# One-hot columns of the expert gates shared among three engines, with eight up tiles in three split passes beside them

## The reference

```
top_s, top_i = lax.top_k(s, PEER_TOPK)
...
idx = jnp.take_along_axis(cand_i, best_j, axis=-1)
gates = jax.nn.softmax(best_s, axis=-1)
...
uc = u_tab[ic]
vc = v_tab[ic]
hdn = jax.nn.gelu(jnp.einsum('cd,chkd->chk', xc, uc), approximate=False) * gc
return jnp.einsum('chk,chkd->cd', hdn, vc)
```

## Time and profile before

| | us |
|---|---|
| median of 3 runs | 1634.44 (1633.93 to 1637.54) |
| the profiled execution, its own time | 1635.94 |
| span of the profile | 1634.1 |
| PE busy | 1593.3 (98%) |
| DVE busy | 1261.5 (77%) |
| ACT busy | 869.6 (53%) |
| POOL busy | 194.7 (12%) |

### The profile page before, as it was taken

One profiled execution on the slowest core, in us unless ns is written; L12 is line 12 of the kernel. 1 busy time (PEld: TensorE's weight loads), 2 busy tenths in 40 slices (PEclk: granted clock), 3 DMA queues, 4 the chain that ended last, 5 costly groups with the idle time before them and its releaser, 6 DMA issues.

```text
span 1634.1 us, 32308 instructions
## 1 busy us (share of the span) xinstructions
PE 1593.3 (98%) x11274; PEld 1413.1 (86%) x11274; DVE 1261.5 (77%) x2678; ACT 869.6 (53%) x1599; POOL 194.7 (12%) x153
## 2 busy tenths in 40 slices
PE   6999999999999999999999999999999999999998
PEld 4887988899988877888888888888899877999998
DVE  6885647859989888788888888888778465688887
ACT  3444230464569854555555555555654246576665
POOL 0020211026600000000000000000048004300000
PEclk9999999999999999999999999999999999999999
DMA  9842137856641388777777777777545661255554
GB/s 359 291 139 88 41 133 259 308 165 199 205 146 63 102 257 255 233 243 236 232 238 237 237 241 236 239 237 242 186 157 170 206 207 40 79 174 185 181 180 128
DMA packets 102623, 316.85 MB, mean 194 GB/s; under 512 B 11392, under 2 KB 21376, under 8 KB 102144
## 3 DMA queue, kind: packets, MB, share of 16 engines
q1 hardware_dynamic: 101664, 311.23, 58.3%
q10 hardware_dynamic: 864, 4.32, 0.7%
HBM read 309.61 MB, written 5.90 MB: 193 GB/s over the span
## 4 chain that ended last, share of the span: by engine, by line
PE 79%; DVE 7%; ACT 7%; POOL 2%; issue 2%; DMA 2%; SPq 0%; DVEq 0%; POOLq 0%; ACTq 0%
PE bank L515 10%; PE bank L502 9%; PE bank L503 8%; PE bank L504 8%; PE bank L2110 7%; PE bank L2112 7%; PE bank L2114 7%; PE bank L523 5%; POOL wlo L496 2%; ACT arena L2073 2%; PE bank L763 2%; PE bank L1746 2%; ACT arena L2064 2%; DVE wlo L496 1%; PE bank L1910 1%
## 5 line engine op out<-in xcount | busy, mean ns | idle before, releaser
L491 ACT CAST whi<-wring 128x1024 fp32r<-128x1024 f32 x395 | 412.7, 1046 | 177.2 <-PE bank L504 109.5
L496 DVE TENSOR_TENSOR wlo<-wring,whi 128x1024 fp32r<-128x1024 f32 x341 | 416.9, 1223 | 63.2 <-ACT whi L491 54.3
L496 POOL TENSOR_TENSOR wlo<-wring,whi 128x1024 fp32r<-128x1024 f32 x54 | 138.0, 2563 | 905.6 <-ACT whi L491 905.5
L502 PE MATMUL bank<-xboth,whi 128*128 128x256 f32 x752 | 219.1, 291 | 6.8 <-POOL wlo L496 2.6
L503 PE MATMUL bank<-xboth,whi 128*128 128x256 f32 x752 | 212.6, 283 | 0.0
L504 PE MATMUL bank<-xboth,wlo 128*128 128x256 f32 x752 | 212.5, 283 | 0.0
L515 PE MATMUL bank<-xboth,whi 128*128 128x512 f32 x704 | 188.7, 390 | 0.0
L2110 PE MATMUL bank<-whi,Whi 128*128 128x512 f32 x512 | 160.2, 394 | 3.8 <-DVE Wlo L2230 3.8
L2112 PE MATMUL bank<-wlo,Whi 128*128 128x512 f32 x512 | 158.6, 391 | 0.0
L2114 PE MATMUL bank<-whi,Wlo 128*128 128x512 f32 x512 | 157.7, 389 | 0.0
L502 PEld LDWEIGHTS bank<-xboth,whi 128*128 128x128 f32 x752 | 143.9, 191 | 13.5 <-issue 6.4
(11 more groups left out here) (397 smaller groups left out, 3094.2 us busy)
## 6 DMA issues: line engine op xcount, KB each, us to landing
wring<-in_w SPq DMA_DIRECT2D x463, 512.0 KB, 3.9
arena<-in_ada SPq DMA_DIRECT2D x48, 512.0 KB, 7.1
xn<-in_ada SPq DMA_DIRECT2D x96, 256.0 KB, 2.9
h_spill<-arena SPq DMA_DIRECT2D x37, 128.0 KB, 2.4
arena<-h_spill SPq DMA_DIRECT2D x37, 128.0 KB, 4.2
wring<-in_w SPq DMA_DIRECT2D x6, 384.0 KB, 5.6
wring<-in_w SPq DMA_DIRECT2D x8, 256.0 KB, 3.2
arena<-in_const ACTq DMA_DIRECT2D x1, 1151.0 KB, 5.1
```

The source lines that it names most:

```text
L491: act.copy(whi[:, n % HSLOTS, :], wring[:, n % SLOTS, :]).then_inc(hi_ready, 1)
L496: eng.tensor_tensor(wlo[:, n % SLOTS, :], wring[:, n % SLOTS, :], whi[:, n % HSLOTS, :].bitcast(F32), ALU.subtract).then_inc(lo_ready, 1)
L502: pe.matmul(out, h, xh, start=start, stop=False, **kw)
```

## The change

Nothing is computed in another way but the eight up tiles 32 to 39 (numbers i = 0 to 7 below), which become split tiles. `A4` and `B4` move to the buffer `xn` of the normed rows, which no later matmul reads then, so that all of `whi` is free for uppers.

Of the four columns `B4[t]` of a group, VectorE, GpSimd and ScalarE now make:

| n mod 4 | VectorE | GpSimd | ScalarE |
|---|---|---|---|
| 0 | t = 0 | 1, 2 | 3 |
| 1 | 0, 1 | 2, 3 | |
| 2 | 0, 1 | 2 | 3 |
| 3 | 0, 1 | 2, 3 | |

That is 112, 112 and 32 of 256 (192, 0 and 64 before). ScalarE makes the uppers of tiles 32 to 34 between the Gelus of tiles 28 to 31, and those of 35 to 39 in groups 6, 14, 22, 30, 38; VectorE makes the lower of tile 32 while it waits for the turned routes, and the other seven behind its columns of groups 1, 6, 14, 22, 30, 38, 46.

```diff
-        rG, _ = region(arena, S * NK + 2 * KT * S + D, [("A4", 1024), ("B4", 1024)])
+        rG, _ = region(xn_flat, 0, [("A4", 1024), ("B4", 1024)])
...
             for j in range(EXP_AFTER, TURN_AFTER):
                 act_early(act, j)
+                if 0 <= j - 28 < HSLOTS:
+                    n = P0 + j - 28 + TURN_AFTER
+                    act_hi(act, n, count_at(n), None)
...
+            n = P0 + TURN_AFTER
+            dve.wait_ge(lo_ready, nth_split[n] - 1)
+            tile_lo(dve, n, nth_split[n])
             dve.wait_ge(t3_turned, 1)
...
-                for t in range(3):
+                for t in range(1 if n % 4 == 0 else 2):
                     ins = dve.tensor_scalar(B4[:, b, t, :], rG["iota"], T3[:, 1, t0 + t:t0 + t + 1],
                                             T3[:, 2, t0 + t:t0 + t + 1], ALU.is_equal, ALU.mult)
                 ins.then_inc(hot, 1)
+                if n in LO_AT:
+                    tile = P0 + TURN_AFTER + LO_AT[n]
+                    tile_lo(dve, tile, nth_split[tile])
+
+        HI_AT = {8 * i - 18: i for i in range(HSLOTS, EARLY - TURN_AFTER)}
+        LO_AT = {max(1, 8 * i - 10): i for i in range(1, EARLY - TURN_AFTER)}
...
+        def pool_hot(pool):
+            pool.wait_ge(t3_ready, 1)
+            for n in range(GROUPS):
+                b, t0 = n % 2, 4 * n
+                if n >= 2:
+                    pool.wait_ge(g_ready, n - 1)
+                for t in (1, 2) if n % 4 == 0 else (2,) if n % 2 == 0 else (2, 3):
+                    ins = pool.tensor_scalar(B4[:, b, t, :], rG["iota"], T3[:, 1, t0 + t:t0 + t + 1],
+                                             T3[:, 2, t0 + t:t0 + t + 1], ALU.is_equal, ALU.mult)
+                ins.then_inc(hot_pool, 1)
...
+        def pe_late_early(pe, j, k):
+            n = P0 + j
+            if k == 0:
+                pe.wait_ge(lo_ready, nth_split[n])
+                pe.wait_ge(h_early, j - 2)
+            mm = three(pe, bank[j % 3][:, 0:S], n, k, xhi[:, k, :], xlo[:, k, :], k == 0, k == KT - 1)
...
-                    pe_early(pe, TURN_AFTER + j, k, k + 1)
+                    pe_late_early(pe, TURN_AFTER + j, k)
                 pe.wait_ge(hot, n + 1)
-                pe.wait_ge(hot_act, n + 1)
+                pe.wait_ge(hot_pool, n + 1)
+                if n % 2 == 0:
+                    pe.wait_ge(hot_act, n // 2 + 1)
...
-                if n + 2 < GROUPS:
+                if n % 2 == 0 and n + 2 < GROUPS:
                     act_hot(act, n + 2)
+                if n in HI_AT:
+                    j = TURN_AFTER + HI_AT[n]
+                    act_hi(act, P0 + j, count_at(P0 + j), P0 + j - HSLOTS + 1)
```

More of the change, by code:

```diff
@@ L74 @@
 EARLY_PLAIN = 14
+EARLY_TURN = 32
 GATE_SPLIT = 7
@@ L482, in build_layer_pair @@
         split_tiles = [FIRST[name] + k for name in SPLIT for k in range(SPLIT2 if name == "w_in2" else COUNT[name])
-                       if k >= SKIP.get(name, 0) or (name == "peer" and k < EARLY_SPLIT and k != EARLY_PLAIN)]
+                       if k >= SKIP.get(name, 0) or (name == "peer" and k != EARLY_PLAIN and not EARLY_SPLIT <= k < EARLY_TURN)]
         nth_split = {n: i + 1 for i, n in enumerate(split_tiles)}
@@ L1894, in act_route @@
                 act_early(act, j)
+                if 0 <= j - 28 < HSLOTS:
+                    n = P0 + j - 28 + TURN_AFTER
+                    act_hi(act, n, count_at(n), None)
         ranks, rank_wide = sem("ranks"), sem("rank_wide")
-        EXP_AFTER, TURN_AFTER = 25, 32
+        EXP_AFTER, TURN_AFTER = 25, EARLY_TURN
         h_early = sem("h_early")
@@ L2036, in dve_hot @@
                 ins.then_inc(hot, 1)
+                if n in LO_AT:
[3 more added lines that the diff above has]
+        LO_AT = {max(1, 8 * i - 10): i for i in range(1, EARLY - TURN_AFTER)}
+        hot_pool = sem("hot_pool")
+        def pool_hot(pool):
[8 more added lines that the diff above has]
+                ins.then_inc(hot_pool, 1)
         def pieces_beside(n):
@@ L2041, in pieces_beside @@
             return [divmod(i, KT) for i in range(first, min(last, (EARLY - TURN_AFTER) * KT))]
+        def pe_late_early(pe, j, k):
[4 more added lines that the diff above has]
+            mm = three(pe, bank[j % 3][:, 0:S], n, k, xhi[:, k, :], xlo[:, k, :], k == 0, k == KT - 1)
+            if k == KT - 1:
+                mm.then_inc(tile_done, 1)
         def pe_gates(pe):
@@ L2058, in act_hot @@
         def act_hot(act, n):
-            t, away = 4 * n + 3, rG["away"][:, (n % 2) * 128:(n % 2) * 128 + 128]
-            if n >= 2:
-                act.wait_ge(hot_act, n - 1)
+            i = n // 2
+            t, away = 4 * n + 3, rG["away"][:, (i % 2) * 128:(i % 2) * 128 + 128]
+            if i >= 2:
+                act.wait_ge(hot_act, i - 1)
             act.activation(away, rG["iota"], ACT.Square, scale=-1.0, bias=T3[:, 1, t:t + 1]).then_inc(away_ready, 1)
-            act.wait_ge(away_ready, n + 1)
+            act.wait_ge(away_ready, i + 1)
             act.activation(B4[:, n % 2, 3, :], away, ACT.Relu, scale=rG["ngate"][:, n:n + 1],
@@ L2069, in act_gates @@
             act_hot(act, 0)
-            act_hot(act, 1)
             for n in range(GROUPS):
@@ L2080, in act_gates @@
                 if n == GROUPS - 3:
-                    act_hi(act, v_tile(0), count_at(v_tile(0)), None)
+                    act_hi(act, v_tile(0), count_at(v_tile(0)), v_tile(0) - HSLOTS + 1)
         P0 = FIRST["peer"]
@@ L2188, in act_peer @@
             weigh(0)
-            act_hi(act, v_tile(1), count_at(v_tile(1)), None)
+            act_hi(act, v_tile(1), count_at(v_tile(1)), v_tile(1) - HSLOTS + 1)
             weigh(1)
@@ L3249, in _ @@
             pool_route(pool)
+            pool_hot(pool)
             pool.wait_ge(lo_ready, nth_split[FIRST["w_in2"] + RAW2 + 2])
```

## The result

The change makes the kernel slower: 1668.42 us (1668.3 to 1670.47, 4 runs) against 1635.01, a ratio of 1.0205 [1.0192, 1.0218]. That is 33.4 us more, and far outside the range that I gave. The profiled execution took 1668.36, of which 1666.2 is the span.

What follows compares the result with a forecast made beforehand. The 64 groups of the gates were taken to run at VectorE's pace, TensorE and ScalarE close behind. Terms -8.6 + 6.3 - 0.5 + 3.4 = +0.6 us on the median 1634.44 gave 1635.0, range 1628 to 1643.

Steps and rivals of the forecast that it cites:

- the price of GpSimd's column: Gates: a GpSimd column priced from a one-pointer multiplication of 0.37, plus an extra of 0.06, costing +3.4 us.
- e: Extra time on each GpSimd column in the gates, bounded between 0 and 0.21 us, taken as 0.06.
- nearest: GpSimd's one-pointer multiplication on 128x128, 0.37 us long alone, taken as closest to the new two-pointer comparison column.
- GpSimd sets the pace: Rival for the gates: half speed in the comparison, e = 0.11, +5.4 us, 1639.8 us in all; chance 0.30.
- my signs of being wrong: Gates: lumps absent from TensorE's waits, GpSimd columns 0.6 and more where VectorE idles, or VectorE's columns grown to 0.5.
- -8.6 + 6.3 - 0.5: Forecast terms before GpSimd's: TensorE's shorter groups -8.6, TensorE's waits at VectorE's lowers +6.3, the stage's ends -0.5 us.
- the lumps of 6.3: Gates: TensorE waits 0.9 us at each of seven lowers on VectorE, because two buffers give no lead; +6.3 us.
- The 0.23: Gates: GpSimd's first column, shut out by `A4` until 0.69, was to end 0.23 us after it, at 0.92.
- I take the exclusion to hold for the data phase only: VectorE and GpSimd shut each other out of SBUF only while data moves, about 0.07 us of a column.
- My rival from that rule: Whole-instruction exclusion in the gates: VectorE's and GpSimd's times add to 1.80 a group, +26.6 us, 1661; chance 0.04.
- ScalarE: ... No cost.: Gates: ScalarE's two groups cost 1.80 in place of 2.64, under 1.10 per group with uppers; no cost.
- TensorE's gain: Gates: split tiles cut TensorE's group from 1.33 to 1.25 us; at TensorE's pace 64 groups would save 8.6 us.

Runs made afterwards that it cites:

- pool_alone: Changed kernel without `A4` and VectorE's columns from group 2 on, two-element memsets standing for the columns, lowers kept: 1644.15 us against 1634.54 before.
- forms: Changed kernel with GpSimd's columns in four operation forms, 16 groups each (is_equal or multiplication first, one or two pointers): 1651.65 us against 1634.54 before.
- no_a4: Changed kernel without VectorE's `A4` from group 2 on, its columns and lowers kept: 1647.64 us against 1635.77 before.
- split_only: Changed kernel with columns shared as before (VectorE three, ScalarE one, GpSimd none), split tiles kept: 1642.69 us against 1634.54, ratio 1.0046.

## Why the prediction was wrong

**Where the 33 us are.** Going from the best of these kernels to the whole change, a step at a time, over 63 groups: the kernel before 1.386; with quick columns, VectorE cleared and ScalarE's column first 1.275 (-7.0); ScalarE's order as it is 1.441 (+10.5); the true operation 1.540 (+6.2); `A4` and VectorE's columns back 1.911 (+23.4). Together +33.1. The order of the steps matters for the shares: beside `A4`, the form alone is worth 0.42 per group (1.911 with the comparison, 1.49 with two multiplications and as many pointers); without `A4`, 0.10. Neither cause alone costs the 33 us: it is a long column that can't begin beside `A4`.

**The step that failed** is the price of GpSimd's column, "From above, twice the time per element adds 0.11 ..., and a second pointer less than the setup of 0.27, say 0.10: e = 0.21" and the choice of 0.06. A column that nothing hinders takes 0.784, not 0.37 + 0.06: e = 0.41, outside my bounds. The pointer (0.08) was well bounded; the operation wasn't. I had treated as "nearest" because the shape and the engine agreed, and let the pair of operations count for at most half speed. No row of before had another pair in one, so the bound should have been far wider.

Of the rivals it was "GpSimd sets the pace" that came, with 0.41 in place of its e of 0.11, and columns over 0.6 where VectorE idles (0.787 in pool_alone) were one of my signs of being wrong.

With e = 0.41 my own sum has 48 x (0.82 - 0.05) = 37 us for GpSimd in place of 3.4, and -8.6 + 6.3 - 0.5 + 37 = +34, near the 33.4 measured. That it comes so near is partly luck: the lumps of 6.3 don't show apart, ScalarE's order (below) isn't in the sum, and the 16 groups with one column, for which it has room, had columns of up to 1.82. The third quarter of forms has a column near the price that I had used (0.44) and runs at 1.49: by an estimate from the paces, 64 x (1.49 - 1.386) = +7 us for the stage, inside my range.

**The wait for `A4`** is the same step again. The sum let a column end 0.23 after `A4`; it ends 0.67 to 0.76 after. The 0.23 was the quick form's: 0.364 alone, of which 0.13 lay beside VectorE's operation and 0.23 behind it. The comparison has 0.12 beside and 0.67 behind, and 0.23 + 0.41 is 0.64. "I take the exclusion to hold for the data phase only" was right in so far as it is short: a column 0.28 under way runs beside `A4`. But it lies at the column's beginning, so that nearly all of the column is still to come when `A4` ends. The Trainium skill (SBUF — State Buffer, SBUF: two separate sides) says that of a two-input VectorE operation and a GpSimd operation that reads SBUF the one that starts first gets the shared ports for its whole instruction, and that the other is fully blocked. Where `A4` or a lower starts first the runs agree, by the 0.67. Where the column starts 0.28 before they don't, with 0.79 and 0.69 side by side, and no column of the gates holds `A4` off for more than 0.09; the measurement decides. My rival from that rule gave 1661 with a chance of 0.04. It isn't what happened either: with columns of 0.774 its own sum is 1.20 + 1.75 x 0.774 = 2.55 per group, 1709 us. The Trainium skill (SBUF — State Buffer, Who interferes with whom) also counts `tensor_scalar` among the operations that can take the shared ports; here VectorE's columns hardly held GpSimd off (a median of 0.786 in no_a4).

**A second error, hidden by this one:** "ScalarE: ... No cost." I compared sums, 1.80 for two groups against TensorE's 2.5. But copy and column stand in one ring with TensorE's products, 2.83 for two groups. With quick columns and VectorE cleared the change still runs at 1.441, and at 1.275 with ScalarE's column first. I had followed the two buffers for VectorE and not for ScalarE.

**What held.** TensorE's gain (1.25 per group; 1.275 seen once nothing else is late); the price of a lower (1.14 in split_only; in the changed kernel VectorE waits for GpSimd's groups anyway, 39.0 us in 47 waits for TensorE, and the lumps don't show apart); VectorE's columns with a median of 0.34, as before; the lower of tile 32, the uppers and the new place of `A4` and `B4` without a visible cost in split_only, which loses no more than its lumps. The first product was to come within 0.3 of 466.83; it came at 468.25, after two GpSimd columns behind two `A4`.

## What to carry to other kernels

Price an operation on GpSimd by a row with the same pair of operations and the same number of pointers; where there is none, the price is open by a factor of two and more (0.36 to 0.79 here). Look which of two engines a common release starts first: a GpSimd column that starts with a two-input VectorE operation, or just before it, is to be added behind that operation, while one that starts 0.28 earlier runs beside it. A kernel that starts its columns that much earlier was not tried. And when work moves between engines, follow each ring (product, copy, column, product) in order, not only each engine's sum.

## What the runs showed of the hardware

- GpSimd's `tensor_scalar` on 128x128 float32 costs by its pair of operations: 0.36 (mult, mult, one pointer), 0.44 (mult, mult or mult, add, two pointers), 0.59 (one operation), 0.70 (subtract, max, one pointer), 0.71 (is_equal, mult, one pointer), 0.78 to 0.79 (the other pairs tried, with two pointers: is_equal, is_ge, min or subtract with mult, and add, add).
- The exclusion is lopsided: beside the gates' columns `A4` stays within 0.68 to 0.78 us, while a GpSimd column that starts with it grows from 0.79 to 1.29, to 1.38 where VectorE's columns follow, and to 1.82 beside a lower. A column that starts 0.28 or more before `A4` is not longer than alone.
- After TensorE's wait of 2.05 at the start of the gates, its granted clock, full until then, had a mean of 0.57 from 468 to 472, so that it ran mostly at 1.2 of its 2.4 GHz; the products took up to 0.55 in place of 0.275. The slow products are part of the 2.3 by which the first copy is late. The windows of the kernel after (columns as above):

```profile
464.00:468.00 4.00, 2.20 (x19) 2.00 (x17) 3.48 (x9) 1.07 (x3) 2.17 (x2) 1.00 0.57 182
468.00:472.00 4.00, 3.75 (x20) 3.78 (x20) 2.25 (x4) 1.38 (x3) 3.79 (x4) 0.57 0.00 0
472.00:476.00 4.00, 2.72 (x25) 2.55 (x23) 2.16 (x5) 1.96 (x4) 3.71 (x4) 1.00 0.00 0
```
